# A block inverse in 32 x 32 products on the four diagonal quadrants

## The chip, the cores and the metric

The kernel runs on one core of one Trainium2 chip. The metric is the device time of one execution in microseconds; lower is better.

## What is computed

One layer of a hybrid decoder trunk for 1024 tokens of width 1024, all in float32. An adaLN-modulated RMSNorm is followed by one wide projection, whose columns feed three branches: a gated linear recurrence (LRU), an RWKV-7 time mixing with 16 heads of 64, and sliding-window attention. The branches are projected, gated, summed and projected again, and a SwiGLU layer ends it. The change is in the RWKV branch, whose recurrence is

```
def step(state, inp):
    r_t, w_t, k_t, v_t, a_t, b_t = inp
    sa = jnp.einsum('bhvk,bhk->bhv', state, a_t)
    state = (state * w_t[:, :, None, :] + sa[..., None] * b_t[:, :, None, :]
             + v_t[..., None] * k_t[:, :, None, :])
    return state, jnp.einsum('bhvk,bhk->bhv', state, r_t)
...
w = -jax.nn.softplus(-(w0 + jnp.tanh(wl) @ w2)) - 0.5
decay = jnp.exp(-jnp.exp(heads(w)))
y = rwkv7_scan(rh, decay, kh, vh, -kk, kk * ah)
```

The kernel does it in 16 chunks of 64 tokens. Within a chunk the tokens depend on each other through a strictly triangular 64 x 64 matrix, and the inverse of (identity minus that matrix) is needed for each chunk and head.

## The kernel before

**Order of the work.** Every engine has its own program, written out by hand, and they meet at semaphores. PE does the products. After a projection for the low-rank inputs comes a loop over 8 pairs of heads (the RWKV loop, 8 turns), a loop of 2 turns for the LRU branch, the attention, the branch projections, and the feed-forward part. Dense products (helper line L246) take three passes in a rounded format, with weights split by POOL. All small products of the RWKV branch are true fp32; each of them leaves two load and two product records in the trace.

**A turn of the RWKV loop.** Six dense blocks, between them the sums over key squares (L715), low-rank products (L719, L720), transposes to token-major form (L740), the products of all token pairs of a chunk (L750), then the inverse (L757 to L787), the matrices of the state's recurrence (L792 to L812), the chain of 16 chunk states (L819 to L838), and a last dense block with transposes (L849). Head 0 of the pair has SBUF and PSUM rows 0 to 63, head 1 rows 64 to 127, so its products are 64 x 64 and come in pairs on separate halves of the array. The 16 chunks are treated in two batches B of 8; a batch is 8 chunks x 2 heads, 16 products, 32 records.

**The inverse.** `am[.., AM_BA, :]` holds the triangular matrix, `xx[:, 0]` the inverse so far and `xx[:, 1]` its transpose; both start as the identity (POOL, L635). At level lv (0 to 5) diagonal blocks of 2^lv tokens are joined to blocks of 2^(lv+1). Level 0 transposes the matrix by a product with the identity (L762). Each level 1 to 5 has, for each batch, y = matrix x inverse into PSUM bank 2 (L772), a copy of its block columns to `y1` on ACT (L1176), then inverse x y into bank 0 (L783, not at the last level) and its transpose into bank 1 (L786), and for each of the two a copy under a level mask back into `xx` on DVE (L1591). The copies name blocks of the level and its mask lets through only the new off-diagonal blocks of 2^lv. Up to level 4 all blocks that count lie in the two diagonal 32 x 32 blocks of each 64 x 64 matrix; level 5 fills the block between them. The order on PE within a level is y of both batches, then the updates of both batches, and each engine waits for counts of the others (`wait_alone` puts a wait in front of a run of products, L210).

Of the kernel before, what the change touches and what calls it, by code (L numbers as in the profile page):

```python
# [37 lines left out]
LEVELS = int(math.log2(CHUNK))  # L38
# [87 lines left out]
def build(nc, a, out):  # L126
    ctx = ExitStack()
    with ctx:
# [28 lines left out]
        ident = keep[:, C_ID:C_ID + P]  # L157
# [50 lines left out]
        def wait_alone(eng):  # L208

            eng.sem_inc(passed[eng.engine.name], 1)  # L210

        def upto(n):

            return max(n, 0) + 1 if isinstance(n, int) else n + 1
# [89 lines left out]
        BATCH = CHUNKS // 2  # L304
# [13 lines left out]
        am = rw["am"].rearrange("p (c q n) -> p c q n", c=CHUNKS, q=4)  # L318
        AM_BA, AM_BR, AM_KA, AM_KR = range(4)
        xx = rw["xx"].rearrange("p (o c n) -> p o c n", o=2, c=CHUNKS)  # L320
        y1 = chunked(rw["y1"])
# [11 lines left out]
        def bank(B, n, rows=slice(0, P)):  # L333

            return ps[rows, 4 * B + (n + 2) % 4, :].rearrange("p (c n) -> p c n", n=CHUNK)
# [138 lines left out]
        def xu_count(i, lv, B, o):  # L474

            return i * N_XU + ((lv - 1) * 4 + 2 * B + o if lv < LEVELS - 1 else (lv - 1) * 4 + B) + 1
# [176 lines left out]
        def _(pe):  # L653
            mm = nc.tensor.matmul
# [20 lines left out]
            for n in range(ADA0):  # L675
                pe.wait_ge(ada_acc, upto(n + 1))
                pe.wait_ge(ada_out, upto(n - 1))
                for c in range(2):
                    ins = mm(ps[:, 2 + n % 2, c:c + 1], ada_acc0[:, n % 2, c * P:(c + 1) * P], ones[:, 0:1], start=True, stop=True)
# [17 lines left out]
            with pe.Fori(0, PAIRS) as i:  # L697
# [3 lines left out]
                for h in range(2):  # L701
                    hs = slice(h * 512, (h + 1) * 512)
                    mm(ps[:, 4 + h, :], rw["lw"][0:64, :], rw["wa"][0:64, hs], start=True, stop=True)
                    ins = mm(ps[:, 6 + h, :], rw["lw"][64:128, :], rw["wa"][64:128, hs], start=True, stop=True)
# [8 lines left out]
                for c in range(CHUNKS):  # L713
                    for hp in HEADS:
                        ins = mm(ps[hp, 4, c:c + 1], rw["bv"][hp, c * CHUNK:(c + 1) * CHUNK], ones[hp, 0:1], start=True, stop=True)  # L715
                ins.then_inc(r_kks, 1)
                for h in range(2):
                    hs = slice(h * 512, (h + 1) * 512)
                    mm(ps[:, 6 + h, :], rw["lg0"], rw["g0"][:, hs], start=True, stop=False)  # L719
                    ins = mm(ps[:, 6 + h, :], rw["lg1"][0:32, :], rw["g1"][0:32, hs], start=False, stop=True)  # L720
# [8 lines left out]
                pe.wait_ge(v_c, upto(i * VC + VC))  # L729
                pe.wait_ge(v_mix, upto(XM0 + i * 6 + 6))  # L730
                pe.wait_ge(a_gate, upto(i * 3 + 2))
                each = [[(c, h, hp) for c in range(B * BATCH, (B + 1) * BATCH) for h, hp in enumerate(HEADS)] for B in range(2)]
                for B in range(2):
                    if B == 1:
# [2 lines left out]
                    for j in range(4 * B, 4 * B + 4):  # L737
                        tok = slice(j * P, (j + 1) * P)
                        for q, src in enumerate((rw["v"], rw["bn"], rw["kt"], al)):
                            ins = pe.transpose(ps[:, j, q * P:(q + 1) * P], src[:, tok], ident)  # L740
                    ins.then_inc(r_tk, 1)
                for B in range(2):
# [3 lines left out]
                    for c in range(B * BATCH, (B + 1) * BATCH):  # L746
                        for src, at in ((rw["bn"], 0), (rw["kt"], 2 * CHUNK)):
                            for hp in HEADS:
                                dst = ps[hp, c // 2, c % 2 * 256 + at:c % 2 * 256 + at + 2 * CHUNK]
                                ins = mm(dst, src[hp, c * CHUNK:(c + 1) * CHUNK], ar[hp, c, :, :], start=True, stop=True)  # L750
                        if c % 4 == 3:
                            ins.then_inc(r_am, 1)
                for B in range(2):
                    pe.wait_ge(v_am, upto(i * 6 + 3 * B + 2))
                    wait_alone(pe)
                    for c, h, hp in each[B]:
                        ins = mm(bank(B, 1, hp)[:, c % BATCH, :], am[hp, c, AM_KA, :], tk[hp, c, TK_V, :], start=True, stop=True)  # L757
                    ins.then_inc(r_ak, 1)
                    pe.wait_ge(v_am, upto(i * 6 + 3 * B + 3))
                    wait_alone(pe)  # L760
                    for c, h, hp in each[B]:
                        ins = mm(bank(B, 0, hp)[:, c % BATCH, :], am[hp, c, AM_BA, :], ident[hp, hp], start=True, stop=True)  # L762
                    ins.then_inc(r_x0, 1)
                for lv in range(1, LEVELS):
                    for B in range(2):
                        if lv == 1:
                            pe.wait_ge(v_x0, upto(i * 4 + 2 * B + 2))
                        else:
                            pe.wait_ge(v_xu, upto(xu_count(i, lv - 1, B, 0)))
                        wait_alone(pe)  # L770
                        for c, h, hp in each[B]:
                            ins = mm(bank(B, 2, hp)[:, c % BATCH, :], am[hp, c, AM_BA, :], xx[hp, 0, c, :], start=True, stop=True)  # L772
                        ins.then_inc(r_y1, 1)
                    for B in range(2):
                        if lv == 1:
                            pe.wait_ge(a_ak, upto(i * 2 + B + 1))
                        else:
                            pe.wait_ge(v_xu, upto(xu_count(i, lv - 1, B, 1)))
                        pe.wait_ge(a_y1, upto(y1_count(i, lv, B)))
                        wait_alone(pe)  # L780
                        if lv < LEVELS - 1:
                            for c, h, hp in each[B]:
                                ins = mm(bank(B, 0, hp)[:, c % BATCH, :], xx[hp, 1, c, :], y1[hp, c, :], start=True, stop=True)  # L783
                            ins.then_inc(r_xu, 1)
                        for c, h, hp in each[B]:
                            ins = mm(bank(B, 1, hp)[:, c % BATCH, :], y1[hp, c, :], xx[hp, 1, c, :], start=True, stop=True)  # L786
                        ins.then_inc(r_xu, 1)  # L787
                for B in range(2):
                    pe.wait_ge(v_xu, upto(xu_count(i, LEVELS - 1, B, 1)))
                    wait_alone(pe)  # L790
                    for c, h, hp in each[B]:
                        ins = mm(bank(B, 3, hp)[:, c % BATCH, :], xx[hp, 1, c, :], tk[hp, c, TK_A, :], start=True, stop=True)  # L792
                    ins.then_inc(r_w, 1)
                    for c, h, hp in each[B]:
                        ins = mm(bank(B, 2, hp)[:, c % BATCH, :], xx[hp, 1, c, :], am[hp, c, AM_KA, :], start=True, stop=True)
                    ins.then_inc(r_w, 1)
                for B in range(2):
                    pe.wait_ge(v_w, upto(i * 4 + 2 * B + 1))
                    wait_alone(pe)
                    for c, h, hp in each[B]:  # L800
                        ins = mm(bank(B, 1, hp)[:, c % BATCH, :], tk[hp, c, TK_A, :], tk[hp, c, TK_B, :], start=True, stop=True)
# [3 lines left out]
                    for c in range(B * BATCH, (B + 1) * BATCH):  # L805
                        for hp in HEADS:
                            mm(bank(B, 2, hp)[:, c % BATCH, :], tk[hp, c, TK_B, :], am[hp, c, AM_KA, :], start=True, stop=False)
                        for hp in HEADS:
                            ins = mm(bank(B, 2, hp)[:, c % BATCH, :], tk[hp, c, TK_K, :], tk[hp, c, TK_V, :], start=False, stop=True)
                    ins.then_inc(r_qmg, 1)  # L810
                    for c, h, hp in each[B]:
                        ins = mm(bank(B, 0, hp)[:, c % BATCH, :], tk[hp, c, TK_A, :], am[hp, c, AM_BR, :], start=True, stop=True)  # L812
# [15 lines left out]
                for c in range(1, CHUNKS):  # L828
# [4 lines left out]
                    if c < CHUNKS - 1:  # L833
                        for hp in HEADS:
                            ins = mm(bank(c // BATCH, 3, hp)[:, c % BATCH, :], qq[hp, c, :], state[hp, :], start=True, stop=True)  # L835
                        ins.then_inc(r_s, 1)
                    for hp in HEADS:
                        ins = mm(bank(c // BATCH, 0, hp)[:, c % BATCH, :], gt[hp, c, :], state[hp, :], start=False, stop=True)  # L838
# [9 lines left out]
                for j in range(T // P):  # L848
                    ins = pe.transpose(ps[:, 4 + j // 4, j % 4 * P:(j % 4 + 1) * P], rw["A"][:, j * P:(j + 1) * P], ident)  # L849
# [20 lines left out]
            with pe.Fori(0, TURNS["lru"]) as g:  # L870
                for c, (kind, j) in enumerate(LRU_ORDER):
# [3 lines left out]
                    if kind == "y" and j > 0:  # L875
                        pe.wait_ge(ada_acc, upto(g * ADA_G + (ADA0 + ADA_PHASE * j)))
                        pe.wait_ge(l_sa, upto(g * (2 * LRU_G) + 2 * j))
                        for q in range(ADA_PHASE):
                            ins = mm(ps[:, 4, q:q + 1], ada_acc1[:, q, :], ones[:, 0:1], start=True, stop=True)
# [136 lines left out]
            for g, (nm, kts, *_) in enumerate(BR):  # L1016
                for i in range(4):
                    for c in range(2):

                        n = g * 8 + i * 2 + c  # L1020
# [4 lines left out]
            for t in range(8):  # L1025
# [3 lines left out]
                for k in range(KT):  # L1029
                    ins = pe.transpose(ps[:, 4 + 2 * (t % 2) + k // 4, (k % 4) * P:(k % 4 + 1) * P], yraw[:, t % 2, k * P:(k + 1) * P], ident)  # L1030
# [10 lines left out]
            for k in range(KT):  # L1041
                pe.wait_ge(m_sq, upto(k + 1))
                for h in range(2):
                    ins = mm(ps[:, 4 + h, :], ones, mt[:, k % 2, h * 512:(h + 1) * 512], start=k == 0, stop=k == KT - 1)
# [36 lines left out]
            for t in range(8):  # L1081
                if t >= 2:
                    pe.wait_ge(m_o, upto(t - 1))
                for k in range(KT):
                    ins = pe.transpose(ps[:, 4 + 2 * (t % 2) + k // 4, (k % 4) * P:(k % 4 + 1) * P], x2[:, k, t * P:(t + 1) * P], ident)
# [821 lines left out]
```

## Time and profile before

| | |
|---|---|
| runs, median (lowest to highest) | 3149.4 us (3149.35 to 3154.89), 3 runs |
| the profiled execution, its time and its span | 3150.59 us, 3148.8 us |
| mean granted TensorE clock | 0.964 of full speed |
| busy: PE, weight load (PEld), DVE, ACT, POOL | 93%, 76%, 46%, 22%, 23% of the span |
| instructions in the trace | 61688, of which 25715 products and 25715 weight loads |
| instruction queue (q8) | 191 packets, 3.13 MB |

PE is TensorE's products, PEld its weight loads, which have records of their own. Busy shares count overlapping records once; the ends of products are modelled. A row of a view says how long an engine was busy with a group, how long one instruction took on average, and how long the engine stood idle before it and what ended that ("issue" is time for which the profile shows no one that was waited for).

### The profile page before, as it was taken

The page shows a single profiled execution, that of the slowest core. Times are in us where ns is not written, and L with a number is a line of the kernel's source. Part 1 is how long each engine was busy: PE and PEld are TensorE (multiplying, and loading weights), DVE is VectorE, ACT ScalarE, POOL GpSimd, SP SyncE. Part 2 cuts the span into 40 slices and gives each one's busy share as a digit, 9 for nine tenths or more (in the row PEclk, how much of TensorE's full clock was granted, in tenths as well). Part 3 has the DMA queues.
Part 4 walks back from the last instruction along what each step waited for, and adds up shares of the span by engine and source line. Part 5 has one row for each costly group of instructions (what it writes and reads, how often), then busy time and mean ns, then how long its engine had stood idle before and what let it go on. Part 6 is the DMA issues. An engine that isn't in the chain of part 4 may idle for free.

```text
span 3148.8 us, 61688 instructions
## 1 busy us (share of the span) xinstructions
PE 2926.4 (93%) x25715; PEld 2385.0 (76%) x25715; DVE 1458.6 (46%) x1801; ACT 706.7 (22%) x1004; POOL 724.0 (23%) x454
## 2 busy tenths in 40 slices
PE   1899999999999999999979988989897999999998
PEld 1687878787888888776757766777685888888886
DVE  6555454555454554675744655445523222222222
ACT  1222121212121221244435664001202000000001
POOL 0212020203021111132312101333231333333331
PEclk7999999999999999999989998999897999999999
DMA  5111111102010110233421102333410111111111
GB/s 179 49 44 35 37 42 31 54 19 70 23 50 29 44 36 29 78 109 88 124 64 38 44 14 83 115 122 128 134 54 27 47 47 53 47 47 47 53 47 67
DMA packets 247066, 192.75 MB, mean 61 GB/s; under 512 B 21729, under 2 KB 225083, under 8 KB 246843
## 3 DMA queue, kind: packets, MB, share of 16 engines
q1 hardware_dynamic: 239136, 163.02, 17.5%
q10 hardware_dynamic: 7707, 26.34, 2.1%
q8 instruction: 191, 3.13, 0.4%
q14 instruction: 32, 0.26, 0.0%
HBM read 158.91 MB, written 30.41 MB: 60 GB/s over the span
## 4 chain that ended last, share of the span: by engine, by line
PE 84%; DVE 8%; ACT 4%; issue 3%; DMA 1%; ACTq 0%; DVEq 0%; POOL 0%; SPq 0%; POOLq 0%
PE ps L246 59%; PE ps L772 2%; PE ps L786 2%; PE ps L783 2%; PE ps L750 2%; DVE arena L1424 2%; PE ps L835 1%; PE ps L866 1%; PE ps L867 1%; PE ps L952 1%; PE ps L977 1%; PE ps L965 1%; DVE arena L1649 1%; PE ps L720 1%; ACT arena L1275 1%
## 5 line engine op out<-in xcount | busy, mean ns | idle before, releaser
L246 PE MATMUL ps<-x_hi,w_hi 128*128 128x512 f32 (+1 forms) x2576 | 839.5, 401 | 49.9 <-DVE x_lo L1850 17.7
L246 PE MATMUL ps<-x_lo,w_hi 128*128 128x512 f32 (+1 forms) x2576 | 821.8, 395 | 0.0
L246 PE MATMUL ps<-x_hi,w_lo 128*128 128x512 f32 (+1 forms) x2576 | 820.0, 394 | 0.0
L236 POOL CAST w_hi<-w_raw 128x1024 fp32r<-128x1024 f32 (+2 forms) x221 | 224.1, 1014 | 2365.4 <-PE ps L246 1629.4
L246 PEld LDWEIGHTS ps<-x_hi,w_hi 128*128 128x128 f32 (+1 forms) x2576 | 485.1, 191 | 189.6 <-issue 66.1
L246 PEld LDWEIGHTS ps<-x_hi,w_lo 128*128 128x128 f32 (+1 forms) x2576 | 489.6, 190 | 106.7
L246 PEld LDWEIGHTS ps<-x_lo,w_hi 128*128 128x128 f32 (+1 forms) x2576 | 490.9, 191 | 104.4
L238 POOL TENSOR_TENSOR w_lo<-w_raw,w_hi 128x1024 fp32r<-128x1024 f32 (+2 forms) x221 | 484.2, 2191 | 17.7
L1856 DVE TENSOR_TENSOR arena<-ps,arena 128x1024 f32<-128x1024 f32 x22 | 26.9, 1225 | 396.3 <-PE ps L246 396.3
L1873 DVE SCALAR_TENSOR_TENSOR arena<-ps,mod,arena 128x1024 f32<-128x1024 f32 x88 | 113.0, 1284 | 129.1 <-PE ps L246 129.1
L1591 DVE COPY_PREDICATED arena<-hid_lo,ps 128x256 f32<-128x256 int32 x144 | 72.0, 500 | 139.8 <-PE ps L783 90.4
L1424 DVE SCALAR_TENSOR_TENSOR arena<-arena,mod 128x128 f32<-128x128 f32 (+1 forms) x280 | 129.0, 461 | 10.0
L1374 ACT ACTIVATE hid_hi<-arena 128x1024 fp32r<-128x1024 f32 x22 | 23.4, 1062 | 450.7 <-PE ps L246 316.9
L246 PE MATMUL ps<-hid_hi,w_hi 128*128 128x512 f32 x352 | 109.1, 391 | 4.8 <-DVE hid_lo L1861 4.8
L246 PE MATMUL ps<-hid_lo,w_hi 128*128 128x512 f32 x352 | 108.8, 390 | 0.0
L246 PE MATMUL ps<-hid_hi,w_lo 128*128 128x512 f32 x352 | 108.8, 390 | 0.0
L1275 ACT ACTIVATE arena<-arena 128x256 f32<-128x256 f32 x128 | 75.4, 591 | 84.4 <-DVE arena L1754 84.4
L786 PE MATMUL ps<-arena 64*64 64x64 f32 x2560 | 89.4, 218 | 0.0
L1504 DVE TENSOR_TENSOR arena<-arena 128x1024 f32<-128x1024 f32 (+1 forms) x27 | 42.9, 1588 | 98.3 <-ACT arena L1120 97.3
L772 PE MATMUL ps<-arena 64*64 64x64 f32 x2560 | 84.5, 218 | 0.7
L786 PEld LDWEIGHTS ps<-arena 64*64 64x64 f32 x2560 | 83.2, 135 | 0.2 <-issue 0.2
L772 PEld LDWEIGHTS ps<-arena 64*64 64x64 f32 x2560 | 80.2, 135 | 1.7 <-issue 1.6
(263 smaller groups left out, 3541.5 us busy)
## 6 DMA issues: line engine op xcount, KB each, us to landing
w_raw<-in_w_in SPq DMA_DIRECT2D x78, 512.0 KB, 3.9
w_raw<-in_w_ffn_in SPq DMA_DIRECT2D x44, 512.0 KB, 3.8
arena<-in_w_ada SPq DMA_DIRECT2D x32, 512.0 KB, 3.8
gates_sig<-arena ACTq DMA_DIRECT2D x24, 512.0 KB, 2.6
arena<-gates_sig SPq DMA_DIRECT2D x24, 512.0 KB, 3.4
w_raw<-in_w_ffn_out SPq DMA_DIRECT2D x22, 512.0 KB, 3.5
arena<-in_x SPq DMA_DIRECT2D x16, 512.0 KB, 5.1
arena<-in_w_ada SPq DMA_DIRECT2D x8, 1024.0 KB, 12.0
```

Of the source, the lines that this page charges most:

```text
L236: nc.gpsimd.tensor_copy(hi, raw).then_inc(s_whi, 1)
L238: nc.gpsimd.tensor_tensor(lo, raw, hi.bitcast(F32), ALU.subtract).then_inc(s_wsplit, 1)
L246: ins = nc.tensor.matmul(dst[h], wp, xp[h], start=first and m == 0, stop=last and m == 2)
L750: ins = mm(dst, src[hp, c * CHUNK:(c + 1) * CHUNK], ar[hp, c, :, :], start=True, stop=True)
L772: ins = mm(bank(B, 2, hp)[:, c % BATCH, :], am[hp, c, AM_BA, :], xx[hp, 0, c, :], start=True, stop=True)
L783: ins = mm(bank(B, 0, hp)[:, c % BATCH, :], xx[hp, 1, c, :], y1[hp, c, :], start=True, stop=True)
L786: ins = mm(bank(B, 1, hp)[:, c % BATCH, :], y1[hp, c, :], xx[hp, 1, c, :], start=True, stop=True)
L1275: fn(sc[:, h, nn, :], sc[:, h, nn, :], ACT.Exp, bias=sm[:, SM_NEG, h, nn:nn + 1], scale=rq[:, gg % 2, t, n0 + nn, h:h + 1], accum_out=sm[: ...
L1424: ins = v.scalar_tensor_tensor(acc, w[:, k, :], c_k, acc, ALU.mult, ALU.add)
L1504: v.tensor_tensor(dst, x0, x1, ALU.subtract).then_inc(v_mix, 1)
L1591: v.copy_predicated(blocks_of(xx[:, o, batch(B), :], lv, o), level_mask(lv, o), blocks_of(bank(B, o), lv, o)).then_inc(v_xu, 1)
L1873: v.scalar_tensor_tensor(r, ps[:, 4 + 2 * (m % 2):6 + 2 * (m % 2), :], mod[:, MOD_G2 + m:MOD_G2 + m + 1], r, ALU.mult, ALU.add).then_inc(m ...
```

## The change

The products of level 0 (L762) and of levels 1 to 4 are made with 32 rows and 32 columns. A 64 x 64 block-diagonal product becomes two 32 x 32 ones, one for each diagonal block, so the four quadrants of 32 rows (two for each head) have one product each. They are issued in the order 0, 2, 1, 3. Each has its quadrant's rows in SBUF as operands, and writes the same rows of PSUM, in columns 0 to 31 or 32 to 63 of the chunk. Level 5 keeps its 64 x 64 products, and no other engine's program changes.

```
+QUARTERS = [(slice(32 * n, 32 * n + 32), slice(32 * (n % 2), 32 * (n % 2) + 32)) for n in (0, 2, 1, 3)]
+diag = [[(c, hp, q) for c in range(B * BATCH, (B + 1) * BATCH) for hp, q in QUARTERS] for B in range(2)]
...
-                    for c, h, hp in each[B]:
-                        ins = mm(bank(B, 0, hp)[:, c % BATCH, :], am[hp, c, AM_BA, :], ident[hp, hp], start=True, stop=True)
+                    for c, hp, q in diag[B]:
+                        ins = mm(bank(B, 0, hp)[:, c % BATCH, q], am[hp, c, AM_BA, q], ident[hp, hp], start=True, stop=True)
...
-                        for c, h, hp in each[B]:
-                            ins = mm(bank(B, 2, hp)[:, c % BATCH, :], am[hp, c, AM_BA, :], xx[hp, 0, c, :], start=True, stop=True)
+                        if lv < LEVELS - 1:
+                            for c, hp, q in diag[B]:
+                                ins = mm(bank(B, 2, hp)[:, c % BATCH, q], am[hp, c, AM_BA, q], xx[hp, 0, c, q], start=True, stop=True)
+                        else:
+                            for c, h, hp in each[B]:
+                                ins = mm(bank(B, 2, hp)[:, c % BATCH, :], am[hp, c, AM_BA, :], xx[hp, 0, c, :], start=True, stop=True)
...
                         if lv < LEVELS - 1:
+                            for c, hp, q in diag[B]:
+                                ins = mm(bank(B, 0, hp)[:, c % BATCH, q], xx[hp, 1, c, q], y1[hp, c, q], start=True, stop=True)
+                            ins.then_inc(r_xu, 1)
+                            for c, hp, q in diag[B]:
+                                ins = mm(bank(B, 1, hp)[:, c % BATCH, q], y1[hp, c, q], xx[hp, 1, c, q], start=True, stop=True)
+                        else:
                             for c, h, hp in each[B]:
-                                ins = mm(bank(B, 0, hp)[:, c % BATCH, :], xx[hp, 1, c, :], y1[hp, c, :], start=True, stop=True)
-                            ins.then_inc(r_xu, 1)
-                        for c, h, hp in each[B]:
-                            ins = mm(bank(B, 1, hp)[:, c % BATCH, :], y1[hp, c, :], xx[hp, 1, c, :], start=True, stop=True)
+                                ins = mm(bank(B, 1, hp)[:, c % BATCH, :], y1[hp, c, :], xx[hp, 1, c, :], start=True, stop=True)
```

## Rows read from the trace of the kernel before

**Rows 1.** Page: the chain that ended last, by engine
```profile
PE 84%; DVE 8%; ACT 4%; issue 3%; DMA 1%; ACTq 0%; DVEq 0%; POOL 0%; SPq 0%; POOLq 0%
```

**Rows 2.** Groups by line: xcount, busy us, mean ns, idle before
```profile
L786 PE MATMUL ps<-arena 64*64 64x64 f32 x2560 | 89.4, 218 | 0.0
L772 PE MATMUL ps<-arena 64*64 64x64 f32 x2560 | 84.5, 218 | 0.7
...
L783 PE MATMUL ps<-arena 64*64 64x64 f32 x2048 | 73.4, 218 | 0.9 <-issue 0.7
...
L762 PE MATMUL ps<-keep,arena 64*64 64x64 f32 x512 | 18.1, 218 | 0.0
```

**Rows 3.** Chain in order of time, 355 to 392 us: start, us, what
```profile
362.15 0.93 PE ps L783 x32
...
365.88 1.87 PE ps L772 x64
367.75 0.93 PE ps L783 x32
```

**Rows 4.** Timeline of one level, 370.5 to 377.3 us
```profile
371.28 2.06 PE L772 MATMUL ps<-arena 64*64 64x64 f32 x64
...
372.45 0.38 ACT L1176 ACTIVATE arena<-ps 128x256 f32<-128x256 f32 x1 [4.28 <-PE ps L772]
...
374.43 0.43 DVE L1591 COPY_PREDICATED arena<-hid_lo,ps 128x256 f32<-128x256 int32 x1 [2.37 <-PE ps L783]
```

**Rows 5.** Timeline of PE at L936, L715 and L750, three windows
```profile
1665.73 1.72 PE L936 MATMUL ps<-keep,arena 128*128 128x2 f32 x14 [1.77 <-ACT arena L1241]
...
309.82 2.03 PE L715 MATMUL ps<-keep,arena 64*64 64x1 f32 x64
...
201.58 7.20 PE L750 MATMUL ps<-arena 64*64 64x128 f32 x128 [0.95 <-DVE arena L1565]
```

**Rows 6.** Windows: us, busy us (instructions) by engine, PEclk, DMA, GB/s
```profile
370.60:386.40 15.80, 15.70 (x540) 15.58 (x537) 4.77 (x11) 2.30 (x6) 0.00 (x0) 1.00 0.02 4
381.37:388.93 7.56, 7.49 (x249) 7.41 (x249) 2.76 (x7) 0.77 (x2) 0.00 (x0) 1.00 0.02 4
388.93:407.62 18.69, 16.91 (x498) 15.72 (x498) 8.97 (x20) 0.00 (x0) 0.00 (x0) 1.00 0.02 4
309.80:311.80 2.00, 2.00 (x66) 1.97 (x65) 1.87 (x2) 1.02 (x1) 1.75 (x1) 1.00 0.03 8
313.00:323.00 10.00, 10.00 (x17) 4.53 (x17) 8.56 (x8) 1.02 (x1) 2.26 (x1) 0.52 0.19 52
```

**Rows 7.** DMA from 370.6 to 386.4 us, 40 slices of 0.395 us
```profile
GB/s 41 0 0 0 0 0 0 0 0 41 0 0 0 0 0 0 0 0 0 0 0 41 0 0 0 0 0 0 0 0 41 0 0 0 0 0 0 0 0 0
...
q8 instruction: 4, 0.07, 1.6%
```

**Rows 8.** Stalls without a releaser: timelines of PEld, chain, L819's idle time
```profile
381.38 0.48 PEld L783 LDWEIGHTS ps<-arena 64*64 64x64 f32 x14 [0.22 <-issue]
...
388.94 0.37 PEld L792 LDWEIGHTS ps<-arena 64*64 64x64 f32 x10 [0.15 <-issue]
...
407.06 0.58 issue
...
  issue: 4.4, 8
```

**Rows 9.** DMA, slices of 0.1 us: 378 to 382 and 404 to 408 us
```profile
GB/s 0 0 0 0 0 0 0 0 0 0 164 0 0 0 0 0 0 0 0 0 0 0 0 0 0 0 0 0 0 0 0 0 0 0 0 0 0 0 0 0
...
GB/s 0 0 0 0 0 0 0 0 0 0 0 164 0 0 0 0 0 0 0 0 0 0 0 0 0 0 0 0 0 0 0 0 0 0 0 0 0 0 0 0
```

**Rows 10.** DMA and PE at the loop's end, 420.3 to 423.5 us, slices of 0.08
```profile
GB/s 205 0 0 0 0 0 0 0 0 0 0 0 0 0 0 0 0 0 0 0 0 0 0 0 0 0 0 0 0 0 0 0 0 0 0 0 0 0 205 0
...
422.86 0.72 PE L246 MATMUL ps<-x_hi,w_hi 128*128 128x512 f32 x2 [0.28 <-issue]
```

**Rows 11.** Instructions of L715: first and last start
```profile
L715 PE MATMUL ps<-keep,arena x512: 193/193/214, 167.2 to 1183.2; 64*64 64x1 f32 x171
```

## The prediction

> **What bounds the kernel now.** I read the page first. The profiled execution has a span of 3148.8 us, and 84% of the chain that ended last lies on PE [rows 1]. So what matters is PE's own time in the stretch that the edit touches. The groups by line give its size: L762, L772, L783 and L786 [rows 2]. Their busy sums contain the overlapping tails of products, so for a duration I go to the chain of one pair of heads [rows 3]: batch follows batch, 32 products each, every 0.93 us (six in 5.60 us between 362.15 and 367.75, 0.933 each), with no wait for DVE or ACT on it. That is 29.2 ns for one product with its weight load. The timeline of one level [rows 4] says why nobody else is late: DVE has finished a copy long before PE is back (a copy is 0.43 us, four of them in a level of 5.6 us), and ACT's 0.38 us lies under PE's next batch. The order on PE is fixed, so a batch that gets shorter or longer moves everything behind it.
>
> A line of the profile holds two records for each fp32 product of the code: L772 has 2560 for 8 pairs x 5 levels x 32 products. Below I count these records.
>
> **What the edit replaces.** Per pair, 2 batches of L762 and 2 + 4 batches in each of the four levels 1 to 4: 26 batches of 32 records, 832 records. In all 6656 records x 29.2 ns = 194 us. Level 5 and everything behind it stay 64 wide. The new code issues 64 records a batch, 1664 a pair, 13312 in all: twice the instructions, each with a quarter of the weights and half the moving columns. It breaks even if a record costs 14.6 ns.
>
> **What a record costs in the array.** Two rows price the weight load. A product with 128 x 128 weights and 2 moving columns takes (1.72 - 0.27) / 13 = 112 ns; one with 64 x 64 weights and a single moving column takes (2.03 - 0.19) / 63 = 29.2 ns, exactly what the level products with 64 moving columns take [rows 5]. So moving columns don't set the 29.2 ns; the weights do: half the columns would be 56 to 58 ns, and two 64-row halves run side by side, which halves it again. Carried on to 32 columns: 112 - 58.4 = 53.6 ns for 64 columns, so 31.6 ns for a 32-column load, and with four quadrants side by side 7.9 ns a record. This is the low bound of the array's price. The high bound is 29.2 ns, no cheaper than now. If quadrants pass only in pairs, it is 15.8 ns. The quadrants are listed 0, 2, 1, 3, so neighbours never share rows; I take 7.9 ns for the array, as the load-limited row is the nearest.
>
> **What a record costs in supply.** This is where I think the edit fails. Between 370.6 and 386.4 us PE executed 540 products and 537 loads [rows 6], and the instruction queue moved 4 packets, in the slices of 370.6, 374.2, 378.9 and 382.5 us [rows 7]. 1077 / 4 = 269 instructions a packet. Three stalls of PE in this pair have no releaser, only "issue" [rows 8]: the loads resume at 381.38 us, they resume at 388.94, and in the state chain PE stands from 407.06 to 407.64. The packets in the slices before the first and the last of them start at 379.0 and 405.1 us [rows 9]: each stall ends 2.3 to 2.5 us after a packet starts. L819 shows the last of these stalls in all 8 pairs, 4.4 us together [rows 8]. Between the first and the second place lie 498 products and loads, between the second and the third 996, twice as many [rows 6]: the stalls come at whole multiples of about 249, which is one packet (waits and register instructions, which the view doesn't list, fill it up). So I read this as PE arriving at the end of what it has and waiting for the next packet, which is asked for only when the one before is in use. Today PE takes some 256 x 14.6 ns = 3.7 us for a packet. How quickly can two follow? At the loop's end, where PE jumps back and also stands still (0.28 us without a releaser, row of 422.86), the two packets are 38 of 40 slices of 3.2 us apart, 3.0 to 3.1 us [rows 10]. None that I found in this kernel lie closer. So the supply is 256 instructions in 3.1 us, 12.1 ns each, 24.2 ns for a load with its product. That is far above 7.9 ns and above the 14.6 ns of break-even.
>
> **The sum.** Per pair the replaced stretch now takes 26 x 0.933 = 24.3 us and one stall of 0.3: 24.6 us. After the change it has 26 x 64 x 2 = 3328 instructions, 13.3 packets at 250 listed instructions each; the first is at least partly there, so I count 13. At 3.1 us each: 40.3 us, +15.7 us a pair, +126 us for 8 pairs. DVE and ACT don't add to it: a level of 768 instructions gets 9.3 us and their work in it is 4 x 0.43 + 2 x 0.38 us. The dense products behind keep their pace, since two products of 512 columns last 0.72 us there [rows 10], so that a packet lasts well over 20 us. Switching between 64-row and 32-row products happens some six times a pair; no row shows one, the nearest is the change from 128-row transposes to L750, which stands 0.95 us, for DVE [rows 5]. I take nothing for it, since PE waits for instructions in this stretch anyway; without that cover the 0.58 us of the long stall of rows 8 as a price, 6 times a pair, would be 28 us. The profiled execution takes 3150.6 us, 1.2 us over the median of the three runs. 3150.6 + 126 - 1.2 = **3275 us**.
>
> The bounds: one packet in 2.9 us (2.4 us from start to use, and some 0.5 us until the next is asked for) gives 37.7 us a pair, +105 us; 3.6 us, as between the packets now while demand sets the pace, gives 46.8 us, +178 us. The likeliest case's own range is 3250 to 3330.
>
> The page "Runtime: NRT & Kernel Launch" of the Trainium skill, section "Instruction fetch mechanics", states that instructions come in blocks of 16 KiB, 256 of them, the next fetched while the current one executes, and that crossing a block costs almost nothing visible. The trace agrees on the block; on the cost, its 0.3 to 0.6 us stalls speak against it already at today's pace. By that rule the sum would be that of the first rival below.
>
> **Rivals.** *Faster: instructions come in time.* If more than one packet can be under way, the array's 7.9 ns decides: a batch of 64 takes 0.51 us. Then a level is not 6 batches but 5 and the hop through ACT (0.25 us from a batch's last start to ACT's, 0.38 in ACT [rows 4], and half of the 0.25 behind it, an estimate from the same row): 3.3 us instead of 5.6, for three levels, and 1.7 us on the fourth, which ends in 64-wide products: 8.3 us a pair, -66 us, **3083 us**. It wins from a packet time under 24.6 / 13 = 1.9 us and gives all of this under 1.1 us. For it speaks that packets themselves are short (1.6% of 16 engines in 15.8 us: 1.0 us each [rows 7]) and DMA is nearly idle here; against it, the stalls and the 3.1 us. 10%.
>
> *Doubling: a record costs what it costs now.* If 29.2 ns is a price per instruction pair, not per load, +194 us: **3343 us**. The equality of 1 and 64 moving columns would fit this as well; the 112 ns of 128 columns doesn't. 6%. The page "TensorE: Matmul & The Clock Gate", Part 1, "Wait — 56ns, not 53.3ns?", says that starts of products never come closer than about 25 ns however few columns they have; by it 13312 records would take 333 us, +139 us, which would be 3288 us and inside my range. The trace's 29.2 ns doesn't contradict that figure.
>
> *The quadrants pass in pairs or in order*, 16 to 19 ns, and supply is not the limit: +19 to +59 us, **3170 to 3210 us**. 5% (and 1% of no change within it).
>
> *The clock falls.* A PE that starves may be granted less. In this trace the clock is 0.52 from 313 to 323 us, right behind 64 one-column products that still had 1.00 [rows 6]; so the lower of the two levels can follow on sparse work, here 1.2 of 2.4 GHz. Against it: the state chain with its gaps, the last of the three long windows, keeps 1.00 [rows 6]. Inside the starved stretch half clock costs nothing (15.8 ns is still below 24.2). Behind it 10 us of 64-wide products at half clock cost 5 us a pair: +40 us on top, **3315 us**. 12%.
>
> The forecast itself has 66%, and 1% more is no change for any reason. Together: faster 0.10, within 0.2% 0.02, slower 0.88; 0.2% (6 us) is about what a measurement of this kernel can tell from no change. The range that leaves out 2 in 10 is 3235 to 3335 us: below it the fast case and the paired quadrants, above it the doubling.
>
> **What would show it.** L762 with 1024 records, L772 with 512 + 4096, L783 4096, the L786 line's products split 4096 and 512. The instruction queue with 191 + 8 x 6.5 = 243 packets, in the level stretch one every 3.0 to 3.2 us whatever PE does. PE idle before these lines for "issue", in gaps of about 1.5 to 2 us that end 2.3 to 2.5 us after a packet's start, and inside a burst 8 to 11 ns between records. From one pair of heads to the next L715 starts every (1183.2 - 167.2) / 7 = 145.1 us now [rows 11]; it would be 161. I am wrong if packets come closer than 2.9 us, if records follow each other evenly at 25 to 29 ns (then the array or the issue is the limit, not supply), or if the granted clock is half in this stretch and behind it. DVE and ACT should wait longer for PE and be no busier.

## The result, and the profile after

The changed kernel takes **3366.0 us** (3356.9 to 3378.9, 4 runs), the kernel before 3152.1 us beside it (3149.35 to 3156.92, 4 runs): **1.069 times** as long, 95% interval 1.065 to 1.073, or 214 us more. The profiled executions differ by 3361.7 - 3150.6 = 211 us. The direction was forecast; the size, 126 us, was not, and 3366 us lies above the top of the range (3335 us).

From one pair of heads to the next it is now (1369.0 - 167.7) / 7 = 171.6 us, where it was 145.1 [rows 11]: 26.5 us a pair, 212 us for eight. So the whole loss lies in the RWKV loop. The page of the profile shows a chain with more "issue" in it (3% before [rows 1]), and the instruction queue, which brings PE's program in packets of 256 instructions, has 246 packets in place of 191:

```profile
q8 instruction: 246, 4.03, 0.5%
...
PE 80%; issue 8%; DVE 7%; ACT 4%; DMA 1%; ACTq 0%; DVEq 0%; POOL 0%; SPq 0%; POOLq 0%
```

```profile
L715 PE MATMUL ps<-keep,arena x512: 193/193/214, 167.7 to 1369.0; 64*64 64x1 f32 x171
```

The groups by line answer to [rows 2]. L790 and L793 are the two updates, L776 is y, L779 and L796 the 64-wide products of level 5, L765 level 0. Columns: busy us, mean ns, idle before them.

```profile
L790 PE MATMUL ps<-arena 32*32 32x32 f32 x4096 | 83.9, 235 | 113.0 <-issue 112.8
...
L793 PE MATMUL ps<-arena 32*32 32x32 f32 x4096 | 71.2, 236 | 0.0
...
L776 PE MATMUL ps<-arena 32*32 32x32 f32 x4096 | 64.8, 226 | 51.3 <-issue 51.3
...
L779 PE MATMUL ps<-arena 64*64 64x64 f32 x512 | 31.5, 313 | 7.5 <-issue 7.5
...
L796 PE MATMUL ps<-arena 64*64 64x64 f32 x512 | 23.6, 272 | 0.0
...
L765 PE MATMUL ps<-keep,arena 32*32 32x32 f32 x1024 | 12.1, 194 | 0.0
```

PE stands 172 us ahead of these lines (113.0 + 51.3 + 7.5), where it stood 1.6 us [rows 2]. All but 0.2 us of it has no releaser: PE waits neither for DVE nor for ACT. The chain of the second pair shows how (start us, us, what):

```profile
387.51 1.43 issue
388.94 1.03 PE ps L776 x66
...
390.45 2.38 issue
392.83 0.65 PE ps L790 x24
393.48 0.85 PE ps L793 x48
394.33 0.45 PE ps L790 x31
394.78 2.07 issue
396.85 0.66 PE ps L790 x33
397.50 0.85 PE ps L793 x64
398.36 0.46 PE ps L776 x30
398.82 1.78 issue
400.60 1.54 PE ps L776 x73
...
433.55 0.98 issue
434.54 2.50 PE ps L779 x42
```

Two microseconds of work, two of nothing, thirteen times. The stalls end at 388.94, 392.83, 396.85, 400.60 and so on up to 434.54: 12 steps in 45.60 us, **3.80 us** each. They don't respect the batches: one falls in the middle of L776, the next in the middle of L790. They add up to 22.4 us of this pair. Each stall ends 2.2 to 2.7 us after a packet's transfer starts (2.4 us in the mean of the thirteen), and the next transfer starts 1.1 to 1.8 us after that end (1.4 us in the mean). And the granted clock was low in it (columns as in [rows 6]):

```profile
346.00:356.00 10.00, 10.00 (x39) 7.00 (x39) 7.82 (x7) 1.03 (x1) 1.53 (x1) 1.00 0.20 52
515.00:525.00 10.00, 10.00 (x18) 5.24 (x18) 7.82 (x7) 1.02 (x1) 1.53 (x1) 0.51 0.19 52
...
1030.00:1040.00 10.00, 10.00 (x19) 5.14 (x18) 8.05 (x7) 1.02 (x1) 1.76 (x1) 0.50 0.19 52
...
387.50:434.50 47.00, 24.57 (x1518) 22.78 (x1518) 8.57 (x17) 3.10 (x8) 0.00 (x0) 0.54 0.02 4
434.50:440.20 5.70, 5.66 (x117) 5.66 (x118) 0.44 (x1) 0.77 (x2) 0.00 (x0) 0.56 0.01 3
```

```profile
169.80:183.50 13.70, 13.70 (x22) 6.45 (x23) 9.57 (x8) 1.02 (x1) 3.29 (x2) 0.50 0.14 38
440.50:513.00 72.50, 70.00 (x892) 58.72 (x888) 40.93 (x51) 16.87 (x18) 14.73 (x8) 1.00 0.13 38
```

The mean granted clock is 0.54 in the four levels and 0.56 in level 5 (the lower level is 1.2 of 2.4 GHz), where it was 1.00 in the first window of [rows 6], which has levels 3 and 4 and most of level 5. The first three rows are the projections behind L719 in three pairs: at 1.00 they take 27.8 us up to the first transposes, with a dip 31.1 to 34.3. Six of the eight pairs have a dip, before two had one: 31.25 us in the mean against 29.04. The last two rows warn against blaming the starved stretch for these dips. The longest one, 34.3 us, is in the first pair, before any 32-wide product has run; and behind the stretch of the second pair the clock is back at 1.00 for 72 us before the next pair's projections dip.

### The profile page after: what moved, and what is told of

It reads as the page before. It is cut to its first block, busy times and chain, and to the rows that moved or that the text cites. A ratio compares the mean times of both kernels' runs of the same rounds, so it can differ in the third digit from the quotient of the medians.

```text
span 3359.9 us, 75000 instructions
## 1 busy us (share of the span) xinstructions
PE 2976.0 (89%) x32371; PEld 2408.4 (72%) x32371; DVE 1454.4 (43%) x1801; ACT 706.8 (21%) x1004; POOL 723.5 (22%) x454
## 4 chain that ended last, share of the span: by engine, by line
PE 80%; issue 8%; DVE 7%; ACT 4%; DMA 1%; ACTq 0%; DVEq 0%; POOL 0%; SPq 0%; POOLq 0%
PE ps L246 56%; PE ps L790 2%; PE ps L776 2%; PE ps L753 2%; PE ps L793 2%; DVE arena L1434 1%; PE ps L845 1%; PE ps L876 1%; PE ps L779 1%; PE ps L877 1%; PE ps L962 1%; PE ps L987 1%; PE ps L720 1%; PE ps L975 1%; PE ps L719 1%
## 5 line engine op out<-in xcount | busy, mean ns | idle before, releaser
L790 PE MATMUL ps<-arena 32*32 32x32 f32 x4096 | 83.9, 235 | 113.0 <-issue 112.8
L1883 DVE SCALAR_TENSOR_TENSOR arena<-ps,mod,arena 128x1024 f32<-128x1024 f32 x88 | 113.0, 1284 | 129.1 <-PE ps L246 129.1
L790 PEld LDWEIGHTS ps<-arena 32*32 32x32 f32 x4096 | 68.8, 145 | 122.3 <-issue 121.1
L776 PE MATMUL ps<-arena 32*32 32x32 f32 x4096 | 64.8, 226 | 51.3 <-issue 51.3
L1186 ACT ACTIVATE arena<-ps 128x256 f32<-128x256 f32 x80 | 30.9, 387 | 366.7 <-PE ps L776 275.5
L776 PEld LDWEIGHTS ps<-arena 32*32 32x32 f32 x4096 | 57.9, 138 | 55.3 <-issue 55.0
```

What stands on the lines that cost most here:

```text
L776: ins = mm(bank(B, 2, hp)[:, c % BATCH, q], am[hp, c, AM_BA, q], xx[hp, 0, c, q], start=True, stop=True)
L790: ins = mm(bank(B, 0, hp)[:, c % BATCH, q], xx[hp, 1, c, q], y1[hp, c, q], start=True, stop=True)
L1883: v.scalar_tensor_tensor(r, ps[:, 4 + 2 * (m % 2):6 + 2 * (m % 2), :], mod[:, MOD_G2 + m:MOD_G2 + m + 1], r, ALU.mult, ALU.add).then_inc(m ...
```

## The experiments

Each kernel ran beside the kernel before, on the same chip; a ratio is to it.

**Padding with increments.** Is it the number of instructions, whatever they are?

```
+                    for _ in range(4):
+                        pe.sem_inc(s_pad, 1)
                     ins = mm(...)            # each 64-wide product of the 26 batches
```

> The kernel before, its 64-wide products untouched, with 4 semaphore increments in front of each product of the 26 batches: 1664 more instructions for PE's queue a pair and not one more for the array, so that PE has as many instructions as after the change. Supply (256 instructions per packet, a packet every 3.8 us as the trace after shows, whatever they are): 13.3 packets, some 49 us for the stretch instead of 24.6, so 3330 to 3370 us, with stalls of PE once in 256 instructions. Doubling (a product with its load costs 29.2 ns at any width): no product was added, so 3149 to 3160 us.

Measured: 5068.5 us, 1.602 (1.592 to 1.611). Neither theory. The trace names the reason, the price of the padding:

```profile
L701 PEldq EVENT_SEMAPHORE  x13312: 51/51/51, 212.0 to 3174.5; - x199
```

(5073.7 - 3148.8) us / 13312 = 145 ns per increment, and the products between four of them start 0.60 us apart. The granted clock is 0.50 in that stretch (window 380 to 400 us). This run says nothing on supply, only that an increment is no cheap filler.

**One pass.** Half the instructions, the same products; the kernel leaves out the lower 16 bits of each float32, and so the precision.

```
+def high(ap): return ap.bitcast(bfloat16).rearrange("p (n two) -> p n two", two=2)[:, :, 1]
-ins = mm(..., am[hp, c, AM_BA, q], xx[hp, 0, c, q], ...)
+ins = mm(..., high(am[hp, c, AM_BA, q]), high(xx[hp, 0, c, q]), ...)   # and the other three
```

> The changed kernel with its 32-wide products made in one pass, from the upper 16 bits of each float32 read as bfloat16: the same products, but half the loads and half the products in the queue, 832 records a pair as before the change (precision is left out). Supply: 6.6 packets x 3.75 us = 25 us, the time of before, so 3145 to 3180 us though the array has work for 9 us only. If the array or a switch between quadrants set the 52 us of the changed kernel, halving the records would leave half of it, 26 us, also; but if the records were only bound by the array at the 10.6 ns that L765 shows in a burst, it would be 3080 to 3090 us.

Measured: 3184.0 us, 1.005 (1.002 to 1.009). The queue has 191 packets again. From the chain:

```profile
519.30 2.59 issue
...
523.78 2.28 issue
...
527.90 1.83 issue
```

The array has little to do, 9.05 us busy in 22.7, and yet nothing is won on the kernel before: the four levels take 23.3 us. The stalls end at 521.89, 526.07 and 529.74, 4.2 and 3.7 us apart, close to the 3.80 of the changed kernel, though these are other instructions. A limit set by the array at 10.6 ns a record (3080 to 3090 us) is out. Copies of DVE and ACT stand on this chain too, between the stalls (0.44 us at 526.56), so the run by itself doesn't show that supply alone sets its time.

**Fill.** Is it the clock?

```
+def fill(lv, n=2):       # behind each batch of levels 1 to 4
+    if lv < LEVELS - 1:
+        for _ in range(n):
+            mm(ps[:, 1, :], x_hi[:, 0, 0:P], x_hi[:, 0, 0:512], start=True, stop=True)
```

> The changed kernel with two more products behind each of its 24 batches in levels 1 to 4, one pass of 128 x 128 weights and 512 columns into a bank that nobody reads: 96 more records a pair, which keep the array busy for about 0.7 us a batch. Supply: the packets' rhythm stays at 3.8 us, the added work lies in the stalls, and what changes is the clock: at 1.00 through the stretch the level 5 products and the next pair's projections get back what half clock took, so 10 to 25 us faster than the changed kernel, 3340 to 3355 us. If PE's own work is what sets the pace of the stretch, 24 x 0.7 x 8 = 134 us slower, 3500 us.

Measured: 3374.8 us, 1.067 (1.060 to 1.074), as the changed kernel's 1.069. The clock came back, the time did not:

```profile
346.00:356.00 10.00, 10.00 (x41) 7.46 (x41) 6.92 (x7) 1.03 (x1) 0.63 (x1) 1.00 0.19 52
387.50:434.50 47.00, 38.47 (x1549) 26.16 (x1550) 7.89 (x16) 3.11 (x8) 0.00 (x0) 0.86 0.02 4
```

With 0.86 in place of 0.54 the same number of records passes in the same 47 us (1549 and 1518). So half clock doesn't set the pace of the stretch. My expectation of a gain failed: from the first product of level 1 to the first one behind level 5 it takes 53.8 us a pair against 51.8, while the projections gain 1.6 us. Added packets don't explain the 2 us, for the whole run has only one more (247 for 246). Fills that don't fit into a stall (two take 1.15 us at half clock) may; it was not taken apart.

**A loop over levels 2 to 4** in PE's program. The same products, but a body that comes round three times.

```
+                def level(lv, last=False):
+                    ...                      # the body as before, waits by the register lv
-                for lv in range(1, LEVELS):
+                level(1)
+                with pe.Fori(2, LEVELS - 1) as lv:
+                    level(lv)
+                level(LEVELS - 1, last=True)
```

> The changed kernel with levels 2 to 4 of PE's program as a loop of three turns over one body of 768 products and loads (three packets), instead of written out three times; all work as in the changed kernel. If instructions that PE has run stay where it can run them again, two of three turns need no packet: 6 packets a pair less, up to 3 x 6 x 3.8 / 3 = 23 us a pair less, 3180 to 3220 us. If every packet is fetched again each turn and the jump adds a stall of its own, 3365 to 3400 us.

Measured: 3230.5 us, 1.020 (1.013 to 1.026), 136 us less than the changed kernel (by the two ratios, each to its own runs of before, some 155 us). 198 packets, 48 fewer, which is six a pair. Windows of the three turns of the second pair:

```profile
385.00:395.90 10.90, 5.62 (x354) 5.33 (x354) 1.21 (x4) 0.77 (x2) 0.00 (x0) 0.50 0.02 5
395.90:401.20 5.30, 4.91 (x401) 4.66 (x390) 1.62 (x5) 0.77 (x2) 0.00 (x0) 0.69 0.00 0
401.20:405.80 4.60, 4.01 (x400) 3.76 (x386) 1.68 (x5) 0.77 (x2) 0.00 (x0) 1.00 0.00 0
```

One and the same code, fetched (last column: some GB/s) 10.9 us, and from what is there (0 GB/s) 5.3 and 4.6. This settles it against doubling: a turn has 6 x 64 = 384 records, which at 29.2 ns each would take 11.2 us in every turn. The time was 10 us over the expectation's upper end.

**Four turns,** level 1 in the loop as well; then **the quadrants in order**. DVE's semaphore `v_xu` starts four higher here, so that the wait of levels 2 to 4, which stands in the body, lets level 1 pass.

```
-                level(1)
-                with pe.Fori(2, LEVELS - 1) as lv:
+                pe.wait_ge(v_x0, upto(i * 4 + 4))     # level 1's waits, for both batches
+                pe.wait_ge(a_ak, upto(i * 2 + 2))
+                wait_alone(pe)
+                with pe.Fori(1, LEVELS - 1) as lv:
```

```
-QUARTERS = [... for n in (0, 2, 1, 3)]
+QUARTERS = [... for n in (0, 1, 2, 3)]
```

> The changed kernel with all of levels 1 to 4 as four turns of one body in PE's program (768 products and loads, all work done; level 1 also waits for both batches' start). In the run with three turns the two later turns took about 4.6 us each without a packet, and the first 11 us. Supply: three turns of four without packets, 9 packets a pair less than the changed kernel, and one more level at 4.6 to 5 instead of 11 us: 50 us below the run with three turns, 3165 to 3195 us.

> The same four turns, but the four quadrants of a chunk issued 0, 1, 2, 3, so that neighbours share a head's rows, where supply doesn't hide what the array takes. If quadrants pass each other freely: the same time as the run before it in this list, within 5 us. If neighbours on one half of the array follow each other as the 64-row halves do (two side by side), a batch takes up to 64 x 15.8 ns = 1.0 us instead of 0.7 to 0.8: 18 batches x 0.25 us x 8 pairs = up to 36 us slower.

Measured: 3187.4 us, 1.010 (1.006 to 1.015), and in order 3181.3 us, 1.009 (1.006 to 1.012). The first expectation holds. The second run shows no price of the order: its batches are the same 0.71 us. The chain of the four-turn run, third turn, and PE's timeline in it:

```profile
378.35 1.44 PE ps L773 x96
379.79 0.11 issue
379.90 0.71 PE ps L784 x46
...
380.80 0.44 DVE arena L1602
381.26 0.71 PE ps L784 x46
...
382.16 0.44 DVE arena L1602
382.60 0.40 issue
```

```profile
378.35 1.44 PE L773 MATMUL ps<-arena 32*32 32x32 f32 x128 [0.42 <-DVE arena L1602]
379.90 0.71 PE L784 MATMUL ps<-arena 32*32 32x32 f32 x62
...
380.47 0.73 PE L787 MATMUL ps<-arena 32*32 32x32 f32 x62
```

Here nothing waits for packets, the clock is 1.00, and the array's price can be read. One record lasts 0.19 us in these rows; without that tail of the last one, records start every (0.71 - 0.19) / 61 = 8.5 ns in L784 and (0.73 - 0.19) / 61 = 8.9 ns in L787. With tail or wait, a batch of 64 takes 0.71 us, 11.1 ns a record: between L773's two batches, which have a wait between them, 0.15 us pass from the last start to the first, where the 64-wide batches of the kernel before have 0.02. And DVE is now on the chain, with a copy of 0.44 us and some 0.3 to 0.5 us around it, twice a turn. A turn takes 4.65 us, where the 64-wide level takes 5.60.

**The same loop with 64-wide products**, first with the waits ahead of it, then with level 1's waits inside the body; the latter with 32-wide products too. `v_xu` starts four higher in all three.

```
                 with pe.Fori(1, LEVELS - 1) as lv:
                     for B in range(2):
+                        pe.wait_ge(v_x0, upto(i * 4 + 2 * B + 2))
...
+                        pe.wait_ge(a_ak, upto(i * 2 + B + 1))
```

> The kernel before, 64-wide products, with levels 1 to 4 as four turns of one body (384 products and loads). Its packets come just as fast as PE uses them, with stalls of 0.2 to 0.6 us at four or five places a pair. Supply: the second to fourth turn need no packet, the stalls behind them shrink or go, 0 to 6 us faster than before (ratio 0.998 to 1.000) unless a jump costs more than it saves. If a turn's jump costs 0.3 us as at the end of the pair's loop: 4 x 0.3 x 8 = 10 us slower, less the stalls.

> The run with 64-wide products and levels 1 to 4 as four turns of one body, but without the wait for both batches ahead of the loop: level 1's waits stand inside the body, where the later turns pass them at once. The trace of the earlier version shows 4.47 us from L762 to the first product of level 1 against 2.80 in the kernel before, 1.67 x 8 = 13 us, which is all that it was slower by, and a turn of 5.73 us against 5.60 written out. So 13 us less: 3150 to 3158 us, even with the kernel before. If the jump itself was what cost, it stays at 3160 to 3170 us.

> The same with the 32-wide products: 13 us less than the earlier version with four turns, 3170 to 3180 us. Per pair three turns at 4.65 us instead of 5.6 (2.9 us gained), a first turn at the pace of its packets, 9.4 us instead of 5.6 (3.8 us lost), L762 0.2 us gained, so 0.7 x 8 = 6 us slower than the kernel before by these terms, and up to 20 us more where the clock is at half in the next pair's projections (31.4 us against 29.0 a pair).

Measured: 3167.4 us, 1.0045 (1.0023 to 1.0068); 3152.8 us, 0.9989 (0.9970 to 1.0008); 3187.8 us, 1.0086 (1.0054 to 1.0118). The first was slower because of my own early wait, as the second, which differs in these waits alone, shows. The chain has it ahead of the first product of level 1:

```profile
367.57 0.73 DVE arena L1584
368.31 0.59 issue
368.90 2.08 PE ps L769 x64
```

With the wait inside it is even with the kernel before, at 158 packets instead of 191: where the supply just keeps up, fewer packets win nothing that can be measured. With 32-wide products the same repair gave nothing, against my expectation. From L765 to the first product of level 1 it is 1.3 us a pair shorter (2.78 for 4.09), but the four turns, of which the first runs at its packets' pace, take 1.85 us longer (25.76 for 23.91): as I read it, the early wait had lain in the shadow of the supply.

**Level 0 alone,** and **half of the steps** (level 0 to 2).

```
-for c, h, hp in each[B]: ins = mm(bank(B, 0, hp)[:, c % BATCH, :], am[hp, c, AM_BA, :], ident[hp, hp], ...)
+for c, hp, q in diag[B]: ins = mm(bank(B, 0, hp)[:, c % BATCH, q], am[hp, c, AM_BA, q], ident[hp, hp], ...)
```

```
-                        if lv < LEVELS - 1:
+                        if lv < 3:           # y and the updates 32-wide in levels 1 and 2
```

> The kernel before with L762 alone as 32-wide products: 64 records more a pair, 128 instructions. The trace after shows its batch shorter (L760 to L765 to L776 takes 3.55 us instead of 3.73), so by the array 1.5 us faster in all. Supply: half a packet more in a stretch that has no slack, 1.9 us a pair less the 0.5 saved: up to 11 us slower, 0 to 11 us.

> Half of the change: L762 and levels 1 and 2 32-wide, levels 3 and 4 64-wide. 14 of 26 batches, 896 more instructions a pair, 3.6 packets. Supply: 3.6 x 3.8 = 13.6 us a pair, 109 us, and up to 15 for the clock behind: 3260 to 3280 us. If the loss came from switching between 64-wide and 32-wide work or from the deeper levels, it would be far from half of the full change's 213 us.

Measured: 3168.3 us, 1.0033 (1.0006 to 1.0060), and 3255.5 us, 1.030 (1.027 to 1.034). Level 0 alone, whose batch is shorter (0.68 us in the chain for 0.93, while the 64-wide batch between its two takes 1.10 for 0.93), makes the kernel slower by 0.33%, some 10 us. Up to the first product of level 1 a pair gains 0.3 us (2.49 for 2.80), but levels 1 to 5 behind it take 28.2 us instead of 26.8. As I read it, they now begin nearer to the end of what PE has. The half change costs 97 us beside its own runs of before, 0.45 of the whole; it was expected at 109 and somewhat more. It has 31 packets more than the kernel before, which makes 97 / 31 = 3.1 us for each, where the whole change has 214 / 55 = 3.9. (The profiled executions give 117 and 211 us and so 3.8 both times, but the half change's is the slowest of its four.) The better measure is the stretch itself, in which the packets can be counted: from the first product of level 0 to the first one behind level 5 a pair takes 29.6 us before, 42.2 in the half change and 54.3 in the whole, with 7.75, 11 and 14 packets in it, 3.8, 3.8 and 3.9 us for each.

**Tiny products** as padding, since the increments had failed.

```
+                    for _ in range(2):      # in front of each 64-wide product of the 26 batches
+                        mm(ps[0:32, 1, 0:2], high(x_hi[0:32, 0, 0:32]), high(x_hi[0:32, 0, 0:2]), ...)
```

> The kernel before, its 64-wide products untouched, with two tiny ones in front of each product of the 26 batches: 32 x 32 weights and 2 columns, one pass, into a bank that nobody reads. That is 1664 more instructions a pair, as in the changed kernel, and little for the array: at the 10.6 ns that a 32-wide record takes in a burst 8.8 us a pair. Supply: 13.3 packets at 3.8 us, 50 us for the stretch, so 3340 to 3370 us. If PE were short of nothing but its array: 3153 + 8 x 8.8 = 3225 us or less.

Measured: 4768.9 us, 1.509 (1.504 to 1.515). Again the padding priced itself. PE's timeline:

```profile
300.63 0.47 PE L782 MATMUL ps<-arena 64*64 64x64 f32 x2
301.04 0.21 PE L703 MATMUL ps<-x_hi 32*32 32x2 bf16 x2
301.17 0.47 PE L782 MATMUL ps<-arena 64*64 64x64 f32 x2
301.58 0.20 PE L703 MATMUL ps<-x_hi 32*32 32x2 bf16 x2
```

One 64-wide product of the code (two records) and two tiny ones take 0.54 us, at a granted clock of 0.50, where the product alone takes 58 ns at 1.00. From the product to the tiny ones 0.41 us pass, back 0.13. Whether the form (64 rows to 32) or the type (float32 to bfloat16) costs this was not taken apart. The changed kernel has a change of form alone, at full clock:

```profile
383.50 1.13 PE L760 MATMUL ps<-arena 64*64 64x64 f32 x32
384.55 0.75 PE L765 MATMUL ps<-keep,arena 32*32 32x32 f32 x64
```

A record of L760 lasts 0.22 us, so 0.14 us pass from its last start (384.41) to L765's first, no more than between two batches of L773. This run, too, says nothing on supply.

## Why the prediction was right in kind and wrong in size

**Which resource limits: right.** PE waits at block ends for instructions. The forecast had 243 packets (246 measured), "issue" ahead of L776 and L790, gaps of about 1.5 to 2 us (1.0 to 2.4) that end 2.3 to 2.5 us after a packet's start (2.2 to 2.7), 8 to 11 ns between records inside a burst (8.5 to 8.9), DVE and ACT no busier. The runs show it twice from opposite sides: the same products without fetching (a turn of 4.6 us instead of 10.9), and half the instructions for the same products (within 1% of the time of before).

**The term that failed: "the supply is 256 instructions in 3.1 us".** It is 3.80 us. I took 3.1 from two packets at the end of the loop, the closest pair that the trace had, and read it as the pace at which packets can follow each other. In the run of fourteen in the second pair none follows closer than 3.3 us. My lower bound shows where the reading failed: 2.4 us from a packet's start to its use were right, but I gave 0.5 us until the next is asked for, and it is 1.4. The other rows that I had, between packets in the level stretch, I took for PE's demand and put into the sum only as the upper bound, as 3.6 us; by my own slices in [rows 7] they are 3.6, 4.7 and 3.6, 4.0 in the mean. That was close to the supply's pace already: the whole stretch has 3.8 us a packet before and after, and [rows 8] has stalls in the levels, just behind them and in the state chain, where a supply with 0.5 us in hand should leave none. With 3.80 us the sum is 13 x 3.80 = 49.4 us a pair in place of 40.3, +24.8 instead of +15.7, 198 us for eight pairs. Measured from the first product of L762 to the first one after level 5, mean of eight pairs: 54.3 us after, 29.6 before, +24.8. So exact an agreement is luck, since I had rounded 13.3 packets down and level 5's slower products are in the measured figure; within 1 or 2 us a pair it stands.

**The clock: the branch that I gave 12% took place in its first half, beside the forecast and not instead of it.** PE that starves is granted half the clock most of the time: 0.54 in the stretch. Half clock in the stretch and behind it was one of my signs of being wrong, yet in the four levels it cost next to nothing, as forecast (the fill run has 0.86 and the same pace). Behind them I had 5 us a pair. Level 5, at 0.56, loses about 2 us, some 118 records in 5.7 us where 128 took 3.7, which the measured stretch contains. From 440.5 us on the clock is 1.00 again. The projections of the next pair lost 2.2 us a pair, 18 us in all, but it isn't shown that the change did it: 6.5 us of the 18 are in the first pair, ahead of every 32-wide product, and the two loops of 64-wide products, whose stretch doesn't starve, have a dip in five pairs of eight (30.9 us in the mean) and in one (28.2), against two in the kernel before. Where the dips fall differs from execution to execution. In the profiled runs 198 + 18 = 216 us, against 211; the rest of the pair became 0.5 us shorter. The range ended too low for the pace first of all: 3.80 us a packet gives 3348 us by my own sum, over the 3335 of the range, with nothing for the clock.

**The array's price: not decisive, and nearly right.** I estimated 7.9 ns a record from the series 112, 58.4, 31.6 ns and four quadrants side by side. Records start every 8.5 to 8.9 ns at clock 1.00. What the fast rival had wrong is what stands around them: with its instructions at hand a level takes 4.65 us, not 3.3, as a batch takes 0.71 us and not 0.51, with its tail and the wait between batches, and DVE's copies come onto the chain. (Its sum also has a slip: three levels at 2.3 us and 1.7 on the fourth are 8.6 us a pair, not 8.3, and the gain of L762 is not in it.) Had all packets come in time, the change would have won (4 x 0.95 + 0.2) x 8 = 32 us, an estimate by these rows, and not 66.

**The other rivals.** Doubling (3343 us) came closer to the measured time than the forecast did, for a wrong reason: 29.2 ns for a record is by accident almost 3.80 us / 128 = 29.7 ns. The total alone could not have told them apart, the loops do. The 25 ns between starts that stood beside it is not there either: 8.5 to 8.9 ns. Quadrants in pairs or in order, at 16 to 19 ns, are out with that, and 0, 1, 2, 3 is as fast as 0, 2, 1, 3. Of the switch between 64-wide and 32-wide work I had said that it hides in the stalls; those at level 0, ahead of the stalls, show nothing beyond the 0.15 us that any wait between 32-wide batches has. The 0.54 us of the tiny products may be the type's and not the form's.

**The rule that I weighed.** The page "Runtime: NRT & Kernel Launch" of the Trainium skill, "Instruction fetch mechanics", has a block boundary all but hidden. The blocks of 256 are there, the hiding isn't: 1.0 to 2.4 us at each of 13 boundaries a pair. It also says that PE's program passes through a FIFO, and that a branch back beyond a window of two blocks forces a fetch. Here a body of 768 products and loads, three blocks, came round three and four times, and only its first turn needed packets; the fetch that the rule wants at each jump back isn't there (0 GB/s in the second and third turn).

No version beat the kernel before; the best one (64-wide products in a loop) is even with it. What stays open is why a packet takes 3.80 us to follow another, when its transfer is about 1 us: why the stall ends only 2.4 us after its start, and why the next one starts only 1.4 us after that.

## What to carry to other kernels

Count instructions as a resource: in code written out, this chip's PE gets 256 of them in 3.8 us, 14.8 ns each, and a float32 product is four. Where products are already at that pace (here 64 x 64 ones, 29.2 ns for a load and a product), splitting them into smaller ones costs what the added packets cost, however little the array has to do. Free of it here was only code that came round in a loop, from its second turn on. And take the pace of a queue from where it is busy for long, not from its closest pair.

## What the runs showed of the hardware

- Packets of instructions follow each other in 3.80 us (12 in 45.60) where PE waits for them, with a granted clock of 0.54 or of 0.86; with bfloat16 products it is 3.7 to 4.2 us.
- PE keeps at least three blocks of code: loop bodies of 768 products and loads needed no packet in later turns. A turn's jump costs little: 5.73 us a turn of 64-wide products against 5.60 written out.
- 32 x 32 float32 products with 32 columns, on four quadrants: a record starts every 8.5 to 8.9 ns at clock 1.00, in either order of the quadrants; a batch of 64 takes 0.71 us from first start to last end.
- A semaphore increment in PE's queue costs 145 ns, at a granted clock of 0.50; alternating 64-row float32 and 32-row bfloat16 products costs 0.54 us for each turn back and forth at half clock.
